# Choosing of the last four expert pieces interleaved with 96 dot products in place of 32, and 16 buffers in place of 14 for the first stream's u rows

## What is computed

```python
def peer(h, w_q, sub_keys, u, v):
    kk = PEER_TOPK                                   # 16, with 8 heads: 128 experts a token
    q = (h @ w_q).reshape(b, l, PEER_HEADS, 2, PEER_KEY_DIM // 2)
    s = jnp.einsum('blhpk,hpnk->blhpn', q, sub_keys).astype(jnp.float32)
    sv, si = lax.top_k(s, kk)
    cand = sv[..., 0, :, None] + sv[..., 1, None, :]
    cv, ci = lax.top_k(cand.reshape(b, l, PEER_HEADS, kk * kk), kk)
    i1 = jnp.take_along_axis(si[..., 0, :], ci // kk, axis=-1)
    i2 = jnp.take_along_axis(si[..., 1, :], ci % kk, axis=-1)
    expert = i1 * PEER_N_KEYS + i2
    gate = jax.nn.softmax(cv, axis=-1).astype(h.dtype)
    ...
        act = jax.nn.gelu(jnp.einsum('tkd,td->tk', u[ex], hx), approximate=False)
        return jnp.einsum('tk,tkd->td', gx * act, v[ex])
```

## Time and profile before

| | us |
|---|---|
| median of 3 runs | 3063.99 |
| lowest, highest | 3062.77, 3068.85 |
| profiled execution, its time | 3068.86 |
| profiled execution, span of the core | 3066.9 |
| busy in the span: TensorE, VectorE, ScalarE, GpSimd | 2335.1, 2206.3, 1266.5, 1274.6 |

### The profile page before, as it was taken

One profiled execution on the slowest core, in us unless ns is written; L12 is line 12 of the kernel. 1 busy time (PEld: TensorE's weight loads), 2 busy tenths in 40 slices (PEclk: granted clock), 3 DMA queues, 4 the chain that ended last, 5 costly groups with the idle time before them and its releaser, 6 DMA issues.

```text
span 3066.9 us, 38874 instructions
## 1 busy us (share of the span) xinstructions
PE 2335.1 (76%) x15054; PEld 2054.5 (67%) x15054; DVE 2206.3 (72%) x2801; ACT 1266.5 (41%) x2063; POOL 1274.6 (42%) x825
## 2 busy tenths in 40 slices
PE   7899999999999899999999950000233329999997
PEld 2588889988888798999997950000132328888886
DVE  1344446877888873444454599999999988989988
ACT  1233334545555563333334320000597924434433
POOL 0000000245555530000000652588788856767763
PEclk8799999999999999999999985555555569999999
DMA  9887776544454459876554367899999978999996
GB/s 377 342 305 292 291 290 216 181 150 158 165 179 139 151 192 358 334 256 238 199 196 165 136 252 289 300 422 422 422 421 421 421 288 294 362 367 376 357 365 237
DMA packets 152794, 868.47 MB, mean 283 GB/s; under 512 B 18865, under 2 KB 31169, under 8 KB 74705
## 3 DMA queue, kind: packets, MB, share of 16 engines
q1 hardware_dynamic: 68578, 449.03, 39.7%
q0 software_dynamic: 73872, 406.08, 34.2%
q10 hardware_dynamic: 10160, 10.88, 1.0%
HBM read 836.81 MB, written 27.39 MB: 282 GB/s over the span
## 4 chain that ended last, share of the span: by engine, by line
PE 46%; DVE 17%; POOL 13%; DMA 11%; issue 9%; ACT 3%; DVEq 0%; SPq 0%; ACTq 0%; POOLq 0%
PE bank L1789 28%; POOL u_ring L734 13%; PE bank L1775 7%; PE bank L2189 4%; DMA v_got<-in_v_rest,expert 4%; DMA raw<-in_tiles 3%; DVE w_lo L1195 3%; PE bank L1814 2%; DMA u_ring<-in_peer_u,expert 2%; DVE u_ring L1649 2%; DVE peer_g L1690 2%; DMA v_raw<-in_v_dense 2%; DVE conv L1309 1%; DVE c_lo L1703 1%; DVE y_w L1367 1%
## 5 line engine op out<-in xcount | busy, mean ns | idle before, releaser
L1195 DVE TENSOR_TENSOR w_lo<-raw,w_hi 128x1024 fp32r<-128x1024 f32 x450 | 600.0, 1347 | 542.3 <-ACT w_hi L779 536.7
L779 ACT ACTIVATE w_hi<-raw 128x1024 fp32r<-128x1024 f32 x482 | 501.1, 1058 | 639.0 <-PE bank L1789 342.1
L1789 PE MATMUL bank<-h_lo,w_hi 128*128 128x256 f32 x2048 | 592.2, 289 | 12.3 <-DVE h_lo L1241 9.0
L1789 PE MATMUL bank<-h_hi,w_lo 128*128 128x256 f32 x2048 | 581.5, 284 | 0.0
L1789 PE MATMUL bank<-h_hi,w_hi 128*128 128x256 f32 x2048 | 581.5, 284 | 0.0
L734 POOL DMA_INDIRECT u_ring<-in_peer_u,expert x256 | 492.6, 1924 | 199.2 <-DVE act_p L1649 120.4
L1649 DVE CUSTOM_DVE_ANT_0 u_ring<-u_ring,h_t 128x2048 f32<-128x2048 f32 x192 | 435.6, 2289 | 21.1 <-DMA u_ring<-in_peer_u,expert 19.4
L741 POOL DMA_INDIRECT v_got<-in_v_rest,expert x256 | 362.0, 1414 | 179.7 <-DVE peer_g L1690 137.3
L1789 PEld LDWEIGHTS bank<-h_lo,w_hi 128*128 128x128 f32 x2048 | 394.6, 193 | 55.3 <-issue 25.3
L1789 PEld LDWEIGHTS bank<-h_hi,w_lo 128*128 128x128 f32 x2048 | 394.9, 193 | 0.9
L1789 PEld LDWEIGHTS bank<-h_hi,w_hi 128*128 128x128 f32 x2048 | 394.5, 193 | 0.0
(11 more groups left out here) (317 smaller groups left out, 4835.7 us busy)
## 6 DMA issues: line engine op xcount, KB each, us to landing
raw<-in_tiles SPq DMA_DIRECT2D x337, 1024.0 KB, 5.5
v_raw<-in_v_dense SPq DMA_DIRECT2D x128, 660.0 KB, 7.3
s_t<-in_states POOLq DMA_DIRECT2D x8, 512.0 KB, 7.3
y_hi_rows<-y_hi_e POOLq DMA_DIRECT2D x16, 256.0 KB, 2.4
y_lo_rows<-y_lo_e POOLq DMA_DIRECT2D x16, 256.0 KB, 6.3
gate_rows<-gate_buf ACTq DMA_DIRECT2D x8, 512.0 KB, 5.3
y_hi<-y_hi_rows POOLq DMA_DIRECT2D x8, 512.0 KB, 8.0
y_lo<-y_lo_rows POOLq DMA_DIRECT2D x8, 512.0 KB, 4.1
```

The costliest lines, as they stand in the source:

```text
L779: act.activation(w_hi[:, i % RING], raw[:, slot % SLOTS, (n % 2) * 2 * CH:(n % 2 + 1) * 2 * CH], ACT.Copy) \
L1195: dve.tensor_tensor(w_lo[:, i % RING], raw[:, n // 2 % SLOTS, (n % 2) * 2 * CH:(n % 2 + 1) * 2 * CH], w_hi[:, i % RING].bitcast(F32), ALU. ...
L1789: ins = pe.matmul(spot if x.shape[1] == KT else spot.rearrange("p (s t) -> p s t", s=NS), w[:, col], moving, start=start and k == 0 and m ...
```

## The change

The dots called at one place of a piece become three (`DOTS`), so the last four pieces hold 4 x 8 x 3 = 96 of the first stream's 128 dots. The first stream goes round over 16 buffers, the old 14 and buffers 17 and 18, and of the first users of the high buffers only that of buffer 16 still waits for the whole first stream.

```diff
@@ ring sizes
+U_EARLY = tuple(range(U_FIRST)) + (17, 18)
+DOTS = 3
@@ ring_slots
         if e < SEL:
-            n = e % U_FIRST
+            n = U_EARLY[e % len(U_EARLY)]
@@ gather_u
                 if U_LAST[e] is not None:
                     pool.wait_ge(u_used, U_LAST[e] + 1)
-                elif U_SLOT[e] >= 2 * U_RING:
+                elif U_SLOT[e] == 16:
                     pool.wait_ge(u_used, SEL)
@@ take
             def take():
-                expert_act(taken[0])
-                taken[0] += 1
+                for _ in range(DOTS):
+                    expert_act(taken[0])
+                    taken[0] += 1
```

## The result

| | us |
|---|---|
| changed kernel, median of 5 runs | 3047.33 (3040.79 to 3051.53) |
| before, the runs beside them | 3063.99 (3062.77 to 3068.85) |
| ratio | 0.9941, 95% interval 0.9927 to 0.9954 |
| profiled execution of the changed kernel, its span | 3040.79, 3038.7 |

A forecast was written before the change was run, and what follows sets the result against it. Expert retrieval was taken as bound by VectorE early, with transfers partly idle, and by full DMA transfers late. Gather 128's rows landing 19 us earlier, with the rest unchanged, gave 3064 - 19 = 3045 us, range 3036 to 3057.

The forecast's parts named there:

- The stretched choosing: Last four choosing pieces: with 24 dots each they take 68.9 us, ending at 2093 us; dots wait for no rows.
- rival E: Gather issues in the choosing: GpSimd is locked out within runs of dots, slower by 16 us, 3080 us; chance 0.04.
- The hand-over: First to second stream: gather 128 issued at 2153.4 us, rows landing at 2158 in place of 2177.2, 19 us earlier.
- What follows the hand-over: Second stream after gather 128: nothing differs, 323 us to the end of the last dot, stage ending at 2481.
- The copies and the buffers: Before gather 128: copies cost 14.1 us, queue almost empty at 2153; two buffers give 5 of the 19 us.
- The waits of VectorE: VectorE's wait for gathered rows over its 256 dots: down from 35.7 us to about 17.
- rival C: Dots of the expert retrieval: VectorE never waits, all 35.7 us gained, 3028 us; chance 0.03.
- What becomes late: Later copies have covers of 57 and 74 us, so no wait; ScalarE done 38 us ahead of the dots.

The follow-up runs named there:

- kernel with more buffers: Against the changed kernel: first stream over 17 to 18 buffers, second stream's first half over eleven, late buffer order changed; 3036.34 us, 0.9909 of before.

## Why the prediction was right, point by point

**The stretched choosing.** Right. The four pieces last 276 us (1810.64 to 2086.5) as the sum said; dots in runs of three never wait for rows, and the first dot that waits for rows is 153, 25 dots behind 128 (predicted: some 30).

**The lock-out of GpSimd (rival E).** Wrong, as the rows had it. The changed kernel's first issues beside runs of three dots, on GpSimd's timeline:

```profile
1811.93 2.71 POOL L736 DMA_INDIRECT u_ring<-in_peer_u,expert  x1 [0.30 <-issue]
1814.94 1.91 POOL L736 DMA_INDIRECT u_ring<-in_peer_u,expert  x1 [0.31 <-issue]
1817.16 1.91 POOL L736 DMA_INDIRECT u_ring<-in_peer_u,expert  x1 [0.30 <-issue]
1819.37 0.94 POOL L736 DMA_INDIRECT u_ring<-in_peer_u,expert  x1 [0.30 <-issue]
```

The three dots start at 1811.54, 1813.76 and 1815.97. One gather comes out for each, delayed to the dot's end, and the next takes 0.94 us again beside the small operations. The Trainium skill (SBUF — State Buffer, "SBUF: two separate sides") has GpSimd blocked until the VectorE operation that holds the shared ports ends. The trace agrees in a mild form: an issue beside a dot takes 1.91 to 2.71 us in place of 0.94, so it is delayed by at most a dot, and the seam between two dots is enough for one gather. The page says this of copies in a 2-port mode, and of operations with two inputs only against a GpSimd operation that reads SBUF; whether that is so of the issue beside a dot, no run here shows.

**The hand-over.** Right, in kind and size. Counted from the start of the fifth piece, gather 128 was to be issued at 333.4 us and its rows to land at 340.5. It was issued at 334.1 and landed 6.6 us later, at 340.7; the issue came 0.7 us later than foreseen and the landing took 0.5 less, so two small errors cancel. The view of this gather alone:

```profile
DMA to landing us min/median/max: 6.6/6.6/6.6
```

**What follows the hand-over.** Here a term was too small. The prediction took over the 323 us from the kernel before, in which the queue is full when gather 128 lands, and that does not hold for a queue that has just run out. Before, gather 132 lands 9.9 us after gather 128, in the changed kernel 12.2; that is 2.3 us lost, and of them 1.9 are still there at gather 255 (321.2 and 323.1 us after gather 128). It fits the 2.7 us of transfers missing at 2145 to 2160, and it is most of the difference between 663.6 us foreseen for the stage and 666.2 measured.

**The copies and the buffers.** The step that failed. The sum 2093 + 46 + 14.1 = 2153 had the queue run out just as gather 128 came, from which followed that two buffers are worth 2 x 2.485 = 5 us. They are worth 2.2 (668.4 - 666.2). With the old 14 buffers gather 124 does land 4.1 us later than with 16 (333.8 and 329.7 us into the stage), and gather 128 3.1 later. But with 14 buffers the queue does not run out: gather 128 is issued at 2150.27 there, lands 9.8 us later, and the stretches around it stay full. In the changed kernel it does run out, so that at gather 132 only 0.8 us of the lead are left.

```profile
2145.00:2150.00 5.00, 0.00 (x0) 0.00 (x0) 5.00 (x7) 0.00 (x0) 0.00 (x0) 0.50 1.01 421
2150.00:2155.00 5.00, 0.00 (x0) 0.00 (x0) 5.00 (x5) 0.00 (x0) 4.12 (x2) 0.50 1.01 419
```

Behind that the distance grows again, to 2.1 us at gather 143; why is open. Nor were the 14.1 us all the price of the copies, as the prediction had it. Of them I expected the h2 copies to be 9, and their absence gave 6.5 in the stage. And the copies fell partly into time that the gathers left unused. In the first 10 us behind the choosing, first before and then without the h2 copies:

```profile
1951.00:1961.00 10.00, 0.00 (x0) 0.00 (x0) 9.61 (x17) 0.00 (x0) 5.59 (x3) 0.50 0.97 243
```

```profile
1949.00:1959.00 10.00, 0.00 (x0) 0.00 (x0) 9.61 (x15) 0.00 (x0) 5.66 (x4) 0.50 0.62 200
```

Without them the transfers stand idle for 38% of this stretch, 3.8 us, or 1.6 MB at 422 GB/s. So of the 5.94 MB that the gathers' queue moved less, part was not taken from it by any copy. What is left for the copies of numbers and gates in small pieces and the first v_raw load was not measured by itself.

**The waits of VectorE.** Predicted 17 us, measured 24.3, although the stage came out. The error is in how I read the view. A dot that waits starts 2.485 us after the one before, 0.27 more than 2.21, but the view counts only 0.18 of idle, because the read of the sum (0.08) then no longer overlaps the next dot. There were 59 waiting dots fewer, 59 x 0.09 = 5.3 us, and 11.4 us less idle: together 16.7, the gain of the stage. For the same reason rival C was undersized: with no wait at all the stage would be 4 x 15.9 + 256 x 2.21 + 3 = 632 us, 51 less than before and not 35.7. The kernel with more buffers took 27 of these.

**What becomes late.** Right. The copies came in time, no dot waited at 128 for gates; ScalarE waited 43.6 us for the last dots where I said 38, since it was done 3.0 us sooner in the stage than foreseen and the dots 2.6 later. Behind the last dot came 561.9 us in place of the 567 of before, which I count as scatter.

## What to carry to other kernels

When a stage is bound by transfers at its end and by an engine at its start, moving engine work so that the transfers are fed evenly can win the idle transfer time; in these runs it won no more than that. Read a pause of the issuing engine against the transfers' own rate in that stretch: here the transfers fell short by 2.7 us in a pause of 17.7, because for most of it the queue was still full. Ring depth pays only if it is carried through: count the buffers at every narrowing, not only where there is room for two more. And when the order of buffers changes, look at what else waits for them: here two loads moved with it, and 3.3 us that looked like the gain of a deeper ring.

## What the runs showed of the hardware that I had not expected

A gather of 1.05 MB issued from GpSimd takes 0.94 us of GpSimd beside short vector operations or when VectorE stands, and 1.91 us with 0.30 between when dots follow each other, so that issues lock to the dots, one for each. In the kernel with four dots eight gathers were issued 1.24 us apart while VectorE stood.

In the 40 us with the copies between partitions, which move 2.4 MB (with the first load of v_raw, in 1024 packets), the gathers' queue moved 5.94 MB less than when alone, two and a half times those bytes; as said above, part of that the gathers would not have moved without the copies either. Without the three h2 copies (1.5 MB), in the 40 us from 1949 to 1989 of that kernel the gathers' queue moved 13.73 MB where it had moved 10.93, which is 2.8 MB back:

```profile
q0 software_dynamic: 1884, 13.73, 85.2%
q1 hardware_dynamic: 784, 0.81, 6.1%
```

A queue of gathers that has run out does not come back at once: the four gathers behind gather 128 took 12.2 us to land in the changed kernel and 9.9 where the queue was full.
